# Other banks for slab 5 and the first gate slab, the last query's norm at another place, and another order of the first loads

## The reference

```
h = rms_norm(x, g_mix); qa,ka,va,qb,kb,vb,ga,gb = split(h @ w_in)
qa,ka,qb,kb = rms_norm per head of 64 (with its own gain)
ya = block attention, 8 heads (blocks of 256, all past blocks kept at this length), causal, relative bias
yb = window attention, 8 query heads on 2 key heads, window 128, one sink logit per head, relative bias
merged = sigmoid(ga + b_a) * (ya @ w_branch_a) + sigmoid(gb + b_b) * (yb @ w_branch_b)
x = x + merged @ w_out
x = x + relu(rms_norm(x, g_ffn) @ w_ff1)^2 @ w_ff2
```

## Time and profile before

| | us |
|---|---|
| median of 3 runs | 678.22 (678.0 to 679.57) |
| profiled execution | 676.66 |
| its span, first to last instruction | 674.9 |
| TensorE busy | 668.8 |
| VectorE, ScalarE, GpSimd busy | 504.8, 370.2, 322.9 |

### The profile page before, as it was taken

The page is one execution under the profiler, slowest core; times in us unless marked ns, Lnnn a source line. Parts: engine busy times, 40 slices in busy tenths (PEclk is TensorE's granted clock), DMA queues, the critical chain, the costliest instruction groups (busy, mean ns, idle before and its releaser), DMA issues.

```text
span 674.9 us, 9472 instructions
## 1 busy us (share of the span) xinstructions
PE 668.8 (99%) x3238; PEld 553.7 (82%) x3238; DVE 504.8 (75%) x701; ACT 370.2 (55%) x662; POOL 322.9 (48%) x194
## 2 busy tenths in 40 slices
PE   9999999999999999999999999999999999999998
PEld 7878787788888888888888888888888888888886
DVE  6667898555555555785559879788797888978897
ACT  7467676676665566543347546254463525536360
POOL 0246676456556653444446436246352454435532
PEclk9999999999999999999999999999999999999999
DMA  8222242222232213555222232414132151220303
GB/s 320 95 93 94 76 128 82 78 81 93 96 94 75 71 45 113 157 181 188 82 93 93 100 118 65 153 62 154 64 113 104 62 186 62 93 101 25 125 0 125
DMA packets 22909, 69.87 MB, mean 104 GB/s; under 512 B 2731, under 2 KB 4011, under 8 KB 22876
## 3 DMA queue, kind: packets, MB, share of 16 engines
q1 hardware_dynamic: 22588, 68.92, 30.3%
q10 hardware_dynamic: 288, 0.52, 0.2%
HBM read 67.27 MB, written 2.16 MB: 103 GB/s over the span
## 4 chain that ended last, share of the span: by engine, by line
PE 94%; DVE 2%; ACT 2%; issue 1%; DMA 1%; POOL 0%; SPq 0%; DVEq 0%; ACTq 0%
PE bank L1375 20%; PE bank L1377 20%; PE bank L1376 20%; PE bank L1692 8%; PE bank L1689 8%; PE bank L1691 8%; PE bank L1476 3%; PE bank L1538 2%; PE bank L1525 2%; PE bank L1559 1%; PE bank L1561 1%; DMA store<-x_t 1%; PE bank L1661 1%; DVE store L1010 0%; PE bank L1404 0%
## 5 line engine op out<-in xcount | busy, mean ns | idle before, releaser
L534 POOL TENSOR_TENSOR w_lo<-w_raw,w_hi 128x1024 fp32r<-128x1024 f32 x77 | 190.2, 2474 | 232.7 <-ACT w_hi L624 232.7
L1375 PE MATMUL bank<-qk_hi,w_hi 128*128 128x512 f32 x320 | 125.0, 391 | 0.0
L1377 PE MATMUL bank<-qk_hi,w_lo 128*128 128x512 f32 x320 | 124.5, 389 | 0.0
L1376 PE MATMUL bank<-qk_lo,w_hi 128*128 128x512 f32 x320 | 124.5, 389 | 0.0
L1375 PE MATMUL bank<-x_hi,w_hi 128*128 128x512 f32 x304 | 122.4, 403 | 1.6 <-DVE v_parts L1016 1.1
L1377 PE MATMUL bank<-x_hi,w_lo 128*128 128x512 f32 x304 | 118.8, 391 | 0.0
L1376 PE MATMUL bank<-x_lo,w_hi 128*128 128x512 f32 x304 | 118.4, 389 | 0.0
L624 ACT ACTIVATE w_hi<-w_raw 128x1024 fp32r<-128x1024 f32 x80 | 83.9, 1056 | 59.4 <-PE bank L1377 55.0
L1258 DVE SCALAR_TENSOR_TENSOR store<-bank,softmax,store 128x512 f32<-128x512 f32 x101 | 72.0, 744 | 23.2 <-PE bank L1692 23.1
L1692 PE MATMUL bank<-v_parts,x_lo 128*128 128x512 f32 (+1 forms) x218 | 84.4, 387 | 0.0
L1689 PE MATMUL bank<-v_parts,x_hi 128*128 128x512 f32 (+1 forms) x218 | 84.4, 387 | 0.0
(11 more groups left out here) (165 smaller groups left out, 1213.1 us busy)
## 6 DMA issues: line engine op xcount, KB each, us to landing
w_raw<-slabs SPq DMA_DIRECT2D x80, 512.0 KB, 3.3
bias_m<-slabs SPq DMA_DIRECT2D x16, 512.0 KB, 3.6
qk_hi_again<-slabs SPq DMA_DIRECT2D x16, 512.0 KB, 5.2
store<-x_t SPq DMA_DIRECT2D x16, 256.0 KB, 3.4
bias_m<-tab_dram SPq DMA_DIRECT2D x8, 256.0 KB, 4.3
out<-store SPq DMA_DIRECT2D x7, 256.0 KB, 2.1
bias_m<-tab_dram SPq DMA_DIRECT2D x8, 128.0 KB, 3.6
w_raw<-slabs ACTq DMA_DIRECT2D x2, 256.0 KB, 3.4
```

Source lines behind the costliest of these rows:

```text
L534: pool.tensor_tensor(w_lo[:, g % WS, :], w_raw[:, g % RAW, :], w_hi[:, g % WS, :].bitcast(F32), ALU.subtract).then_inc(w_lo_ready, 1)
L1375: pe.matmul(out_, wh, xh, start=first, stop=False)
L1376: pe.matmul(out_, wh, xl, start=False, stop=False)
L1377: last = pe.matmul(out_, wl, xh, start=False, stop=end)
```

## The change

Slab 5 goes to bank 5 and waits for `ms_ready` instead of `va_lo(0)`; the first gate slab goes to bank 6 and waits for slab 13's read instead of slab 15's. Slab 16's head sum comes after kt 5 of slab 17 instead of kt 6; its mean comes ahead of slab 15's norm on DVE; its root ahead of `split_hi(19)` on ACT instead of in step 1; its norm in step 0, behind the second maximum, instead of in step 2. PE's transposes of the second head of step 0 get a wait for the first gate slab's read. SP issues x's tile 0 ahead of the parameters, and ACT rounds the first weights ahead of its wait for the parameters.

```diff
         def acc(g):
-            return bank[(0, 1, 2, 6, 7)[g % 5]]
+            return bank[5 if g == N_VA + 1 else (0, 1, 2, 6, 7)[g % 5]]
+        def gate_bank(j):
+            return bank[0 if j else 6]
...
# SP, the first loads
-            sp.dma_start(par[:, :], params).then_inc(par_arrived, 16)
             for k in range(KT):
+                if k == 1:
+                    sp.dma_start(par[:, :], params).then_inc(par_arrived, 16)
...
# ACT
+            hi_part(0, slice(0, FIRST * P), first_arrived[0])
             act.wait_ge(par_arrived, 16)
             for k in range(KT):
-                if k == 0:
-                    hi_part(0, slice(0, FIRST * P), first_arrived[0])
...
             for g in range(N_VA, N_QKV):
+                if g == LAST_V:
+                    qkv_root(LAST_Q)
                 split_hi(g + 2)
...
                     exps(step)
-                if step == 1:
-                    qkv_root(LAST_Q)
...
# DVE
                     v_scale(g)
+                if g == LAST_Q:
+                    qk_mean(g)
                 if N_VA <= g - 1 < LAST_Q:
                     qk_norm(g - 1)
-                if not is_v(g):
+                if g < LAST_Q:
                     qk_mean(g)
...
             def gate_scale(j):
-                dve.tensor_tensor(store[:, j, :], bank[0][:, :], r_all[:, :],
+                dve.tensor_tensor(store[:, j, :], gate_bank(j)[:, :], r_all[:, :],
...
-                if step == 2:
-                    qk_norm(LAST_Q)
                 for e in range(2):
...
                         scores_max(*units(step)[e])
+                    if step == 0 and e == 1:
+                        qk_norm(LAST_Q)
...
# PE
             def table_product(h):
-                    pe.wait_ge(ms_ready, 1)
+                    qkv_read(N_VA + 1)
...
-            AFTER[LAST_V, 6] = LAST_Q
+            AFTER[LAST_V, 5] = LAST_Q
             for g in range(N_VA, N_QKV):
                 pe.wait_ge(w_lo_ready, g)
-                if g >= 5:
-                    qkv_read(g - 5)
+                if g == N_VA + 1:
+                    pe.wait_ge(ms_ready, 1)
+                elif g > N_VA + 1:
+                    qkv_read(0 if g == 10 else g - 5)
...
             def probs_transpose(step):
+                    if u == 1:
+                        pe.wait_ge(acc_read, read(G_GATE))
...
             def gate_part(j, kts, stop):
-                    if j:
+                    if j > 1:
                         pe.wait_ge(acc_read, read(g - 1))
                     else:
-                        qkv_read(g - 3)
-                last = slab_part(g, bank[0], from_x, kts, kts[0] == 0, stop)
+                        qkv_read(LAST_Q - 1 if j else LAST_Q - 3)
+                last = slab_part(g, gate_bank(j), from_x, kts, kts[0] == 0, stop)
```

## The result

The change makes the kernel slower, by about half a per cent. In nine runs of each the median went from 677.61 to 681.69 us, ratio 1.0057 (95% interval 1.0044 to 1.007). Timed again beside its parts (six runs) the ratio was 1.0042 (1.0028 to 1.0055). The forecast, 679.5 us within 676.5 to 681.2, had the sign and most of the path; the time fell outside, and the measured loss, 4.1 us, is three times the forecast 1.26. The profiled execution took 680.35 us, its span is 678.6: 3.7 above that of before.

A forecast was written before the change was run, and what follows sets the result against it. TensorE bounds the kernel, busy 668.8 of 674.9 us. The terms -0.15 - 0.65 - 0.31 + 2.70 - 0.33 sum to +1.26 us, put on the median of 678.22: 679.5 us, range 676.5 to 681.2.

The forecast's parts named there:

- A: Start of the kernel: tile 0 issued sooner lets PE's real work begin earlier, -0.15 us (ends -0.35 and +0.3).
- B: Slab 5 in bank 5: its stall goes, part returns as a wait for L996 at slab 4's head sum, -0.65 us.
- C: First gate slab in bank 6: its wait for L1046 of slab 15 goes, -0.31 us.
- D: Slab 16's norm sooner: DVE's refine meets POOL and delays step 2, +2.70 us, with -0.33 us back at L1111.
- Steps 1 to 6: Slab 16's chain: earlier head sum, root, DVE refine stretched beside POOL, late `v_split_lo`, PE starts step 2 +2.70 us.
- Step 7: Step 3: with no norm left on DVE in step 2, the wait for L1111 goes, -0.33 us.
- third rival: PE's new gap at 121 to 123.7 us lowers the clock to 1.2 GHz: up to +3.0, 682.5 us, chance 0.1.
- B's ends: Limits given for slab 5's gain: -1.38 us (nothing late) and -0.3 us.
- the ends of D: Limits for step 2's stall: 0 if DVE and POOL never met (`v_split_lo` over at 120.8), or +3.2 us.

The follow-up runs named there:

- e7: The kernel before with only the two edits of the start (tile 0 ahead of the parameters, first weights rounded earlier); 676.89 us, ratio 0.9999.
- e8: The changed kernel without slab 16's four moves, and slab 4's head sum one kt into slab 6; 676.47 us, ratio 0.9986.
- e3: The changed kernel, but POOL waits with slab 19's low part until DVE's refine of slab 16 is done; 677.04 us, ratio 0.9999.
- e5: The changed kernel with only DVE's norm of slab 16 back in step 2; 676.7 us, ratio 0.999.
- b1: The kernel before, unchanged, run once more for its trace; last product +1.59 us against the shift at 350 us.
- e4: The changed kernel with ten extra unused products ahead of PE's waits for step 2; 677.63 us, ratio 1.0004.
- g1: The changed kernel with four extra unused products ahead of PE's waits for step 2; 678.21 us, ratio 1.0016.
- e6: The changed kernel once more, timed beside its parts; 679.9 us, ratio 1.0042.
- e2: The kernel before with only the four moves of slab 16 (head sum, mean, root, norm); 679.39 us, ratio 1.003.
- e1: The changed kernel with the four moves of slab 16 undone, banks and start as changed; 677.22 us, ratio 1.0002.
- f1: The changed kernel with slab 16's norm back in step 2 and slab 4's head sum one kt into slab 6; 676.21 us, ratio 0.999.

## Why the prediction was right and wrong

*A, the start.* Forecast -0.15, measured -0.11 at the first product. With tile 0 issued 0.44 us sooner the first weights landed later: ACT rounds them at 4.42 instead of 3.62. So `x_hi(0)` starts at 4.95, 0.1 us sooner, and not the parameters but the weights were last (parameters seen by DVE at 4.58). The rule of the Trainium skill (DMA: Bandwidth & Descriptors, "Issuing engines are not separate DMA queues") says that loads issued by SP and ACT share their engines, which would be the cause, and the trace agrees as far as it goes: 0.80 us of slip. The times show nothing of the start (e7), and the -0.32 at 28 us is within what the kernel before does by itself.

*B, slab 5.* Forecast -0.65, by the trace -0.61, with the wait for L996's successor as forecast (0.89 us between two products). Right; e8 shows that the other half could be had.

*C, first gate slab.* Forecast -0.31, measured -0.32. The added wait for its read cost nothing.

*D, the norm.* Steps 1 to 6 are what happened. All of them ran 0.9 to 1.2 us earlier than written, because what A, B and C gain was not taken off their times; the durations and the stall agree within 0.15 us: L984 2.55 long (forecast 2.65), L987 1.67 (1.7), stall of step 2 2.56 (2.70). The forecast named `v_split_lo` as the last to come; the view names the maximum, which is over at 121.8, but `v_split_lo` ends at 122.42 and PE starts at 122.63. e3 shows that the meeting with POOL, not the amount of work, is the cause, and e5 that the norm's place alone brings it. The rule of the Trainium skill (SBUF — State Buffer, "Who interferes with whom"), that issue order decides, held at both instructions, in e8 at a third pair 0.07 us apart, and in b1 with DVE ahead by 0.08. Step 7 gave 0.57 back instead of 0.33.

**The step that failed is the third rival's: "the clock falls in the new gap". It was left out of the sum, given a chance of 0.1 and priced at up to +3.0.** The mean clock was 0.995 to 0.997 in all 15 runs of the changed kernel, and full again in all 21 runs with products in the gap (e4, g1). The price in the sum's own terms was 1.52 us in the first trace, 1.60 in e6's and 1.57 in e2's: the lower level lasted 3.4 us each time, not the "some 6 us" read from the start. I set the chance by the longest gap with a full clock, 1.5 us; a gap of nearly twice that had nothing in its favour, and 0.1 was far too low.

With this term the sum is 2.3 us (+1.26, +1.52, and -0.5 from small errors of the others), 680.5 us, as the ledger has it up to 350 us. That would have been inside the stated range, so the clock alone doesn't put the time outside; what else did is told below. The forecast also stood on a median of three runs, 678.22, which nine runs put at 677.61: 0.6 us in its favour, by luck.

*The range.* It ended at 681.2, for which no working is shown, below that rival's own 682.5. B's ends and D's upper one give 678.8 to 680.4 for the forecast alone, not 678.4 to 680.7. And in the ends of D, `v_split_lo` at 120.8 is 0.8 us later than before, not 2.1, though the stall of 0 follows from the 120.8.

*What no term had:* the last 1.40 us of the profiled execution. The change is not needed for them: the gaps stand in six of 14 traces, two of the three of the kernel before among them, and exactly in those whose landing took 6.2 to 6.7 us, not in the eight with 4.7 to 5.2. There DVE comes 2 us late, its L1205 meets POOL's L534 (3.43 instead of 1.22 us), and PE waits in the last chunk. Both traces of the changed kernel have it; whether it meets late landings more often than the others is not shown. With up to 1.6 us from this and 0.6 from the clock's rise, it is a part of why equal kernels differ by 2 us and more from run to run.

*Left open:* the first ratio, 1.0057, is 3.9 us, the second 2.8; the trace accounts for 2.3 up to 350 us. In three of the nine runs of the first set the mean clock was 0.995, which is about 3.4 us more at the lower level; but the other six have a median of 681.0, still 3.4 us up. How much of the rest is late landings was not separated. The traces of e1, e3, e5 and f1 likewise show more gain than their times. Nor was the gap length found at which the clock falls: it stayed up with 1.5 and 1.73 us, and with 1.89 behind four fillers, fell in five of ten runs with 2.05 and in all with 2.8.

## What to carry to other kernels

Before work of two SBUF inputs is moved on DVE, lay it beside POOL's timeline in the new order: here 1.4 us of refining took 4.2, and it stood ahead of something that PE needed. Count a new gap of TensorE twice, once as a wait and once for the clock behind it, unless the trace has a gap as long with a full clock. A move that fills an engine's idle stretch (the root on ACT) can be free where the next link of the same chain is not; take such chains apart and run the links apart. Before shifts of under 1 us are compared between two traces, take off what lies ahead of the first changed place: here it differed by up to 0.7 us.

## What the runs showed of the hardware that was not expected

- With four unused products, 0.23 us apart, ahead of a gap of 1.89 us the clock stayed up in ten of ten runs (g1); without them, at 2.80 us, it fell in 15 of 15.
- Behind the gap the lower level lasted 3.4 us in all three traces that have it. It began with PE's restart in one (122.6 us) and 1.3 and 1.5 us behind it in the others (e2, e6), at the same price of 1.5 to 1.6 us.
- The rise of the clock at the start comes at another moment in each run: between traces with the same start the products at 28 us differ by up to 0.6 us (the kernel before's start) and 0.7 (the changed one, e8 aside).
- The same two loads of 512 KB, issued behind two others of that size and with next to no other traffic beside them (0.02 of 2.11 MB), took 4.7 to 5.2 us to land in eight traces and 6.2 to 6.7 in six.
- Of a DVE instruction with two SBUF inputs and POOL's subtraction the one issued second was stretched, whichever it was: DVE took 2.55 instead of 0.69 us 0.41 behind POOL, POOL 3.41 instead of 2.40 us 0.08 behind DVE (b1).
